# Four first units of one k each, and six instead of seven products of ones, ahead of a two-block transformer kernel

## The reference

```
h = rmsnorm(x, attn_norm_g[l])
proj = jnp.einsum('bsd,de->bse', h, w_in[l])
qa, ka, va, qb, kb, vb = jnp.split(proj, split_pts, axis=-1)
```

## Time and profile before

| | |
|---|---|
| three runs | 1001.82, 1002.22, 1003.26 us |
| profiled execution, its own time | 1003.34 us |
| its span | 1002.0 us |
| TensorE busy | 976.3 us (97%), 4772 matmul records |
| VectorE busy | 719.2 us (72%) |
| ScalarE busy | 527.7 us (53%) |
| DMA | 214.64 MB, mean 214 GB/s |

### The profile page before, as it was taken

One profiled execution on the slowest core, in us unless ns is written; L12 is line 12 of the kernel. 1 busy time (PEld: TensorE's weight loads), 2 busy tenths in 40 slices (PEclk: granted clock), 3 DMA queues, 4 the chain that ended last, 5 costly groups with the idle time before them and its releaser, 6 DMA issues.

```text
span 1002.0 us, 12880 instructions
## 1 busy us (share of the span) xinstructions
PE 976.3 (97%) x4772; PEld 805.3 (80%) x4772; DVE 719.2 (72%) x1073; ACT 527.7 (53%) x811; POOL 57.4 (6%) x62
## 2 busy tenths in 40 slices
PE   8997999999999999999989999999999989999998
PEld 6876788888788888888878788877888868888886
DVE  5966778888776767777759978677658766566653
ACT  6675654554436444444457845467565474443531
POOL 3310100000000000000000022021000000000000
PEclk9998999999999999999999999999999999999999
DMA  7930648888885888688745766875555727754861
GB/s 250 295 126 1 229 154 269 273 280 263 286 286 186 267 266 263 203 274 304 249 135 190 251 179 191 260 254 167 174 177 204 229 103 242 238 189 137 271 205 49
DMA packets 116428, 214.64 MB, mean 214 GB/s; under 512 B 9042, under 2 KB 16490, under 8 KB 116110
## 3 DMA queue, kind: packets, MB, share of 16 engines
q1 hardware_dynamic: 116222, 213.73, 65.5%
q10 hardware_dynamic: 144, 0.10, 0.0%
HBM read 212.71 MB, written 2.13 MB: 214 GB/s over the span
## 4 chain that ended last, share of the span: by engine, by line
PE 88%; DVE 6%; ACT 2%; DMA 2%; issue 1%; POOL 0%; SPq 0%; ACTq 0%; DVEq 0%
PE ps L1140 26%; PE ps L1142 26%; PE ps L1141 26%; PE ps L1190 3%; DVE wlo L1807 2%; PE ps L1232 2%; PE ps L1277 1%; DMA raw<-in_w_mix 1%; PE ps L1258 1%; ACT whi L1445 1%; PE ps L1168 1%; DMA raw<-in_w_in 1%; DVE qkT L2243 1%; PE ps L1326 1%; PE ps L1328 1%
## 5 line engine op out<-in xcount | busy, mean ns | idle before, releaser
L1445 ACT ACTIVATE whi<-raw 128x1024 fp32r<-128x1024 f32 (+1 forms) x306 | 313.5, 1032 | 295.6 <-PE ps L1142 224.5
L1807 DVE TENSOR_TENSOR wlo<-raw,whi 128x1024 fp32r<-128x1024 f32 (+1 forms) x306 | 361.7, 1195 | 85.9 <-ACT whi L1445 84.6
L1140 PE MATMUL ps<-whi,hTh 128*128 128x512 f32 (+1 forms) x832 | 326.8, 393 | 3.4 <-DVE wlo L1807 3.4
L1142 PE MATMUL ps<-whi,hTl 128*128 128x512 f32 (+1 forms) x832 | 316.2, 380 | 0.0
L1141 PE MATMUL ps<-wlo,hTh 128*128 128x512 f32 (+1 forms) x832 | 316.0, 380 | 0.0
L1140 PEld LDWEIGHTS ps<-whi,hTh 128*128 128x128 f32 x832 | 156.6, 188 | 34.5 <-DVE wlo L1807 4.9
L1142 PEld LDWEIGHTS ps<-whi,hTl 128*128 128x128 f32 x832 | 156.6, 188 | 30.9
L1141 PEld LDWEIGHTS ps<-wlo,hTh 128*128 128x128 f32 x832 | 156.9, 189 | 27.1 <-issue 0.5
L2149 DVE SCALAR_TENSOR_TENSOR aacc<-araw,cs,aacc 128x512 f32<-128x512 f32 x126 | 94.3, 749 | 2.5
L2391 POOL TENSOR_TENSOR stat<-stat,mhalf 128x8 f32<-128x8 f32 (+3 forms) x29 | 36.1, 1255 | 640.4 <-DVE stat L1823 482.0
L1140 PE MATMUL ps<-whi,uh_ffn 128*128 128x512 f32 x176 | 69.3, 394 | 0.0
(11 more groups left out here) (253 smaller groups left out, 1083.6 us busy)
## 6 DMA issues: line engine op xcount, KB each, us to landing
raw<-in_ffn_w_in SPq DMA_DIRECT2D x80, 512.0 KB, 4.5
araw<-in_w_ada SPq DMA_DIRECT2D x72, 512.0 KB, 4.8
raw<-in_w_mix SPq DMA_DIRECT2D x64, 512.0 KB, 4.5
raw<-in_ffn_w_out SPq DMA_DIRECT2D x44, 512.0 KB, 4.9
raw<-in_w_up SPq DMA_DIRECT2D x32, 512.0 KB, 4.6
raw<-in_w_down SPq DMA_DIRECT2D x32, 512.0 KB, 4.7
raw<-in_w_out SPq DMA_DIRECT2D x16, 512.0 KB, 4.2
raw<-in_w_in SPq DMA_DIRECT2D x14, 512.0 KB, 5.8
```

The costliest lines, as they stand in the source:

```text
L1140: pe.e.matmul(o, ah, h[:, j, :], start=s0, stop=False, skip_group_check=True)
L1142: r = pe.e.matmul(o, al, h[:, j, :], start=False, stop=s1, skip_group_check=True)
L1445: act.e.activation(uflat(whi, u), uflat(raw, u), ACT.Copy).then_inc(hi.up(u), 1)
L1807: v.tensor_tensor(uflat(wlo, u), uflat(raw, u), uflat(whi, u).bitcast(f32), SUB).then_inc(lo_dve.up(u), 1)
```

## The change

The block `qa` has eight slices of k. Before, its units hold 1, 1, 2, 2 and 2 of them, five units. After, they hold 1, 1, 1, 1, 2 and 2, six units. All later units keep their content, and their numbers go up by one. The first eight loads are thus `qa`'s six units and the first two of `ka`, where they were `qa`'s five and the first three of `ka`. And TensorE begins with six products of ones, so with twelve records where it had fourteen.

```
-        block(key, "w_in", 0, 8, c0, n, "attn", small=2 * (key == "qa"))
+        block(key, "w_in", 0, 8, c0, n, "attn", small=4 * (key == "qa"))
...
         pe.wait_ge(*made_ident("ones"))
-        for _ in range(7):
+        for _ in range(6):
             pe.e.matmul(ps[7][:, 0:128], ones[:, 0:128], ones[:, 0:128], start=True, stop=True)
```

## The result

The change made the kernel slower by 5.8 us: median 1007.82 us (six runs, 1005.82 to 1010.82) beside 1002.02 for the kernel before (six runs, 1000.55 to 1003.26). The ratio is 1.0059, 95% interval 1.0045 to 1.0074. The profiled execution of the changed kernel took 1010.82 us, the longest of its six, with a span of 1009.4, so a comparison of the two traces shows 7.4 us.

The account below looks back on a forecast made before the run. TensorE bounds the kernel (busy 976.3 of 1002.0 us), its start a transfer. The start's +0.15 us and 0 for ones, loads and modulation steps, on the median 1002.22, gave 1002.4 us; range 1000.4 to 1004.3.

Parts of the forecast that it names:

- When k2 lands: Start, load of k2 alone: lands at 9.48 us, between 8.8 and 10.14; k3 at 10.14.
- ScalarE's queue: Start, ScalarE's copies: net 0.5 us saved; with the earlier landing the sums of squares start 1.2 us earlier, at 15.0.
- VectorE's queue: Start, VectorE: "lo 3" 13.8 to 14.5, "lo 4" ends 16.1, "lo 5" 18.3 to 19.55.
- TensorE: `qa`: the 1.43 us wait returns as waits of 0.8, 0.2 and 0.6; last start 22.15 for 22.00, 0.15 us later.
- Rival 1: `qa`: "lo 3" to "lo 5" aren't late, idle time is kept, last start 20.4; 1.6 us gained, 1000.6; chance 0.17.
- One product of ones less: Kernel's start: 0 for the sum; at most a 0.48 us gain, a loss only through the clock.
- Rival 2: Start, and possibly 85 to 100 us: TensorE's clock rises later, slower; together 1005.2; chance 0.08.
- Loads moved: Third unit of `ka` behind the ten small loads, `qb`'s third unit's load later: cost 0, both covered.
- Modulation steps: "ada" steps come two halves earlier: taken as 0, bounds -1.5 to +1.5 us for each of two or three stage ends.
- Rival 4: "ada" steps, late `b_ada` row or stage ends: fall badly, 1005.4, or well, 999.4; chance 0.08 slow, 0.07 fast.

Follow-up runs that it names:

- e5: Changed kernel with one gate step of the modulation put back behind the residual of `down0`, all others left; 1004.53 us, ratio 1.0035.
- e1: Changed kernel with the planner's count started two lower, so every modulation step stands where it stood before the change; 1002.44 us, ratio 0.9998.
- e8: Changed kernel with the old count and "lo 3" to "lo 5" moved ahead of what held them up on VectorE; 1000.65 us, ratio 0.9989.
- r12: e8 with the `b_ada` rows loaded early as in r11; 1001.34 us, ratio 0.9998.
- e3: Kernel before the change with six products of ones for seven, nothing else; 1002.29 us, ratio 1.0003.
- e4: Changed kernel with the seventh product of ones put back; 1007.28 us, ratio 1.0063.
- e2: Kernel before the change with the planner's count started at +2, nothing else changed; 1008.67 us, ratio 1.0067.
- r11: Changed kernel with the `b_ada` row loaded at the first quarter of its block, not the last; 1006.56 us, ratio 1.0044.
- e6: Changed kernel with the first SwiGLU's end sum at count 287 instead of 284 and the step of 285 left out; 1007.36 us, ratio 1.0065.
- r10: Changed kernel with the old count to the MLP's end and the new one from the first SwiGLU on; 1010.39 us, ratio 1.0083.
- e7: Changed kernel with the edits of e5 and e6 together; 1005.75 us, ratio 1.0045.

## Why the prediction was wrong

It said 1002.4 us and no measurable change; it is 1007.8.

*When k2 lands, ScalarE's queue, VectorE's queue, TensorE.* Right in the main. k2's copy started at 9.45 us for a forecast of 9.48. Where the clock was at full (e5), the first sum of squares began at 15.11 (forecast 15.0), "lo 5" at 18.44 (18.3), the waits were 0.36, 0.62 and 0.60 us (none, 0.8 and 0.2, 0.6), the last start 22.34 (22.15). The 0.2 was a slip: from the 14.5 at which "lo 3" was to end, another 1.23 us of "lo 4" make 15.7, not 16.1, and in e5 it ends at 15.77 and nothing waits for it. The idle time was handed back, as said, and e1 shows the total: no difference. Rival 1 would have needed another order on VectorE, and e8, which gives it that, gets a part of its 1.6 us: 0.8 less in the last start, and 0.1% in the time. With the full clock at the start (r12) the same order gets all of it there, 20.17 for 22.00, where rival 1 said 20.4.

*One product of ones less.* Right on the mean (e3, e4). Rival 2 did come true in the profiled execution of after, with transposes of 1.91 us and 1.27 us later at the end of `qa`, but e3 was at the lower clock until 14 as well, e8 from 8.8 to 12.2, and e4, which has all seven products, from 7.8 to 11.2. The traces are too few to say how often each kernel has it; what e3 and e4 show is that it makes no difference in the medians. The Trainium skill, "TensorE: Matmul & The Clock Gate" (Part 1), has it that the moment of the rise shifts from run to run, by about half a microsecond. That it shifts, the traces bear out, but by far more: the record of the granted clock begins its first stretch at full at 14.1 us in after and at 6.0 in e5, which does the same work up to there.

*Loads moved.* Nothing in any trace speaks against the 0.

*Modulation steps.* This is the step that failed: "I take 0, bounds -1.5 to +1.5 for each of two or three stage ends". By e2 it is +6.1 us in the medians and +6.7 by the ratio. Rival 4 had the mechanism (a late `b_ada` row ahead of something that TensorE needs, at 1005.4) with a chance of 0.08 and half of the price. Three things were wrong in the step.

First, I asked how many steps move and how long one is, and not behind which instruction each lands. Two halves earlier brings no wait that shows for most of the 91 steps; it was costly for one gate step that passed the residual of `down0`, one sum that passed into the narrow block, and, as far as the waits tell, one or two at stage ends. The first could be foreseen from the trace of before: the earlier trace rows show another gate step's row 4.21 us late, at the place itself VectorE waited 1.42 us for its row (277.35, above), and the kernel's order shows that the residual of `down0` stood next to it.

Second, the steps of the first SwiGLU were miscounted. "The rest one number lower" gives it no step more; by the planner's list it does 30 where it did 29. The one at the count 284 stands where before had none, and it is the column sum, with nothing but the narrow block ahead of it.

Third, I priced a wait at its own length. One row of 5.47 us on VectorE became 8.51 on ScalarE and then a string of late loads. And in the profiled execution the 1.88 us of idle time at 449 cost another 1.6 at the lower clock, though in e4 the 2.00 us there cost nothing more.

What stays open: how much of these belongs to each place. The stages' lengths in the traces, measured between the same transposes as above, as differences to before:

```
                            MLP     first SwiGLU    mix
old count: e1, e3, e8       0.0     -0.4 to +0.1    -1.2 to -0.2
new count: after           +2.1     +4.2            +0.7
new count: e2              +3.5     +1.5            -0.8
new count: e4              +3.3     +2.6            -0.7
after with e5's edit       +0.9     +1.3             0.0
after with r11's edit      +0.9     +1.4            +0.5
```

So with the new count the MLP and the first SwiGLU are longer in all three traces, by 5 to 6.3 us together, and how they share it differs from one to the next. In e5 and r11 both stages are shorter than in after, and so the 2.4 us of e5 aren't the MLP's alone. Neither e6 nor r10 separates the 449 place, because both shift what comes later.

## What to carry to other kernels

Where a planner places side work by a running count, an edit anywhere ahead shifts all of it: list the moved steps with the instruction that each now stands before on its in-order engine, and look at those that wait for a load first. Test such a change with the count held (e1) before the edit itself is judged, and the count alone (e2) beside it. And when a wait is taken away at one place, move what is next in the queue too (e8), or the time is handed back a few microseconds later.

## What the hardware showed that I had not expected

After an idle time of only 1.88 us TensorE's clock went to 0.50 for 3.4 us (after, 451.0 to 454.4), and so it did after 3.15 us in r10 (450.4 to 453.8), after 1.94 us at 812.29 in after, and after 2.37 us at 807.91 in r11. Waits of 1.32 us (293.61) and 1.37 us (513.26) were not followed by it, nor was every longer one: e2 waited 1.94 us near 293, e4 2.03 near 293 and 2.00 at 449, r10 2.07 at 512.29 and e7 2.12 at 807.94, all at full clock behind it. So the length of the wait alone doesn't decide; what does is open. The stretch at 813 cost next to nothing: TensorE of before waits 1.43 us for `hTl` at 811.81, 7 us behind the same transposes, and in after the slower matmuls fill that wait, so that the last stage takes 197.1 us in both.

The page's clock row doesn't show the start: it reads full speed in the first slices of after, while matmuls are 0.43 us apart instead of 0.23. There the spacing has to be read.
